# First in-projection of a hybrid encoder as Strassen's seven products, tokens fed in columns

## The chip, the cores and the metric

One core of one Trainium2 chip. The metric is the device time of one execution in microseconds (us); a few runs were made of each kernel, and their median is quoted.

## The reference

Two layers over 2,304 tokens (2,048 of one request, 256 of another) of width 1,024. The part around the change is the first layer's input projection, the rest uses its results:

```python
h = rmsnorm(x, attn_norm[j])          # x * rsqrt(mean(x*x) + eps) * g
proj = h @ w_in                       # (2304 x 1024) @ (1024 x 4096)
q, k, v, z = jnp.split(proj, 4, axis=-1)
# then differential attention of q, k, v; gate by silu(z); output projection;
# then a Fourier layer of the same make
```

All of it is float32 in and out.

## The kernel before, in words

The kernel is a sequence of stages with a barrier between them; a tile's name begins with its stage: `ia` (this projection), `pa` (attention), `oa` (its output projection), `fg` and `fl` (the Fourier layer's gate and transform), `of` (the last output projection). Each engine has its instructions written out in program order; semaphores alone tie the engines together. Float32 accuracy comes from three passes (`three_pass`, lines 206 to 208): each operand is kept as a rounded high part and the rest, its low part, and high x high, low x high and high x low are added in PSUM.

`project_resident` is the stage that is replaced. SP loads 18 blocks of 128 tokens in rows. For each, ACT squares and sums a row and takes the root (lines 442, 444), DVE inverts it, POOL scales the row by it (line 357), PE transposes it (line 399), DVE multiplies by the norm's weight on its way out of PSUM (line 483), ACT rounds it to `xh` (449), and DVE (488) or POOL (361) subtracts to get `xl`. All tokens then stay in SBUF. The weights come in 32 blocks of 128 columns, 512 KB each, loaded by POOL's own DMA queue; POOL makes both parts of each (lines 348 and 352). For each block there are five groups of tokens, four of 512 and one of 256, each of 8 x 3 matmuls. ACT copies a result out of PSUM (line 463, with Silu for `z`), for q and k DVE subtracts to get the low part (line 505), and SP stores. The first groups of tokens are multiplied while later ones are still being made.

## Time and profile before

| | us |
|---|---|
| median of 3 runs | 3052.32 (3045.8 to 3053.98) |
| profiled execution, first to last instruction (its span) | 3051.8 |
| PE busy | 2933.4 (96%) |
| PE weight loads | 2465.4 (81%) |
| DVE busy | 1464.9 (48%) |
| ACT busy | 1339.9 (44%) |
| POOL busy | 790.1 (26%) |

The span is that of the profiled execution; its device time is not listed apart from the three, and the nearest of these is 3052.32, 0.5 above the span. Matmuls are pipelined and their recorded durations overlap, so a rate is read from the distance between starts, not from a duration. Busy shares are means over the stages.

### The profile page before, as it was taken

To read this page: it belongs to the slowest core of one execution; us is meant where nothing else is said; L and a number is where in the kernel's file an instruction comes from. 1 tells how busy PE (TensorE), PEld (TensorE's weight loads), DVE (VectorE), ACT (ScalarE), POOL (GpSimd) and SP (SyncE) were. 2 spreads that over 40 slices of the span, in tenths; PEclk is the share of its full clock that TensorE was granted. 3 is DMA by queue.
4 is the path that set the end of the run, shared out by engine and by line. 5 is a ranking of instruction groups with operands and counts; after the bars stand their busy time and mean duration, and the time that the engine had idled before them with its cause. 6 is when DMAs were issued, how large, how long until landed. Compare 5 with 4: busy or idle time off the path is not lost. (4 is left out here: it accounts for less than half of the span.)

```text
span 3051.8 us, 41686 instructions
## 1 busy us (share of the span) xinstructions
PE 2933.4 (96%) x15038; PEld 2465.4 (81%) x15038; DVE 1464.9 (48%) x1678; ACT 1339.9 (44%) x2348; POOL 790.1 (26%) x414
## 2 busy tenths in 40 slices
PE   7999999999989999999999999998899899899799
PEld 6888888888868787878787888887688899887687
DVE  5111110000068787878787878887787200441322
ACT  6111111111167777777777777775443321221321
POOL 6211111111012222222222222222665221130642
PEclk9999999999989999999999999999899999999899
DMA  6333332242155313232323222120664622565752
GB/s 212 131 114 120 113 107 71 67 116 69 54 135 163 85 56 75 67 71 63 78 63 75 67 61 72 36 88 25 215 207 153 216 91 76 151 172 177 264 177 106
DMA packets 225779, 340.22 MB, mean 111 GB/s; under 512 B 21819, under 2 KB 171515, under 8 KB 220124
## 3 DMA queue, kind: packets, MB, share of 16 engines
q1 hardware_dynamic: 220860, 320.96, 33.5%
q0 software_dynamic: 4736, 16.91, 2.1%
q8 instruction: 103, 1.69, 0.2%
q14 instruction: 80, 0.66, 0.1%
HBM read 224.55 MB, written 125.97 MB: 115 GB/s over the span
## 5 line engine op out<-in xcount | busy, mean ns | idle before, releaser
L1017 DVE TENSOR_REDUCE pa_half_max<-pa_score 128x1 f32<-128x1024 f32 x512 | 625.4, 1222 | 232.5 <-PE pa_score L805 232.5
L951 ACT ACTIVATE pa_p<-pa_score,pa_neg_max 128x1024 f32<-128x1024 f32 x512 | 567.9, 1111 | 75.1 <-DVE pa_neg_max L1023 71.5
L864 PE MATMUL pa_o_acc<-pa_wt,pa_vv 128*128 128x256 f32 x2048 | 511.5, 380 | 1.0 <-ACT pa_o_out_s L986 0.3
L1108 POOL TENSOR_SCALAR pa_p<-pa_p,pa_inv_sum,pa_lam_neg 128x2048 f32<-128x2048 f32 x128 | 262.7, 2052 | 944.7 <-DVE pa_inv_sum L1044 944.7
L801 PE MATMUL pa_score<-pa_ka,pa_qa 128*128 128x512 f32 x1024 | 455.1, 444 | 20.4 <-ACT pa_p L951 9.9
L206 PE MATMUL ia_acc<-ia_xh,ia_wh 128*128 128x512 f32 (+1 forms) x1280 | 472.0, 369 | 1.1 <-DVE ia_stage L505 1.1
L207 PE MATMUL ia_acc<-ia_xl,ia_wh 128*128 128x512 f32 (+1 forms) x1280 | 471.4, 368 | 0.0
L208 PE MATMUL ia_acc<-ia_xh,ia_wl 128*128 128x512 f32 (+1 forms) x1280 | 471.1, 368 | 0.0
L805 PE MATMUL pa_score<-pa_kb,pa_qb 96*128 96x512 f32 x1024 | 422.0, 412 | 0.0
L931 ACT ACTIVATE pa_wt<-pa_turned 128x512 f32<-128x512 f32 x512 | 306.0, 598 | 260.4 <-PE pa_turned L833 259.2
L864 PEld LDWEIGHTS pa_o_acc<-pa_wt,pa_vv 128*128 128x128 f32 x2048 | 367.4, 191 | 44.9 <-ACT pa_o_out_s L986 2.1
L463 ACT ACTIVATE ia_stage<-ia_acc 128x512 fp32r<-128x512 f32 (+3 forms) x160 | 89.0, 556 | 662.0 <-PE ia_acc L208 648.6
L833 PE MATMUL pa_turned<-pa_ident,pa_p 128*128 128x128 f32 x2048 | 314.7, 276 | 10.5 <-ACT pa_wt L931 9.5
L833 PEld LDWEIGHTS pa_turned<-pa_ident,pa_p 128*128 128x128 f32 x2048 | 238.7, 140 | 90.3 <-ACT pa_wt L931 49.4
L1055 DVE SCALAR_TENSOR_TENSOR pa_p<-pa_p,pa_inv_sum 128x2048 f32<-128x2048 f32 x128 | 300.3, 2346 | 0.1
L206 PEld LDWEIGHTS ia_acc<-ia_xh,ia_wh 128*128 128x128 f32 x1280 | 241.6, 189 | 41.7 <-ACT ia_stage L463 1.3
L207 PEld LDWEIGHTS ia_acc<-ia_xl,ia_wh 128*128 128x128 f32 x1280 | 241.6, 189 | 39.9
L208 PEld LDWEIGHTS ia_acc<-ia_xh,ia_wl 128*128 128x128 f32 x1280 | 241.4, 189 | 40.1
L801 PEld LDWEIGHTS pa_score<-pa_ka,pa_qa 128*128 128x128 f32 x1024 | 196.1, 191 | 64.7 <-ACT pa_p L951 20.6
L805 PEld LDWEIGHTS pa_score<-pa_kb,pa_qb 96*128 96x128 f32 x1024 | 196.3, 192 | 32.8
L505 DVE TENSOR_TENSOR ia_stage<-ia_acc,ia_stage 128x512 fp32r<-128x512 f32 (+1 forms) x80 | 51.0, 638 | 319.2 <-ACT ia_stage L463 319.2
L526 DVE TENSOR_TENSOR pa_lam_prod<-pa_lam_vec 128x128 f32<-128x128 f32 x1 | 0.3, 291 | 407.2 <-DMA pa_lam_vec<-attn_lambda_k 407.2
(260 smaller groups left out, 4173.0 us busy)
## 6 DMA issues: line engine op xcount, KB each, us to landing
ia_raw<-attn_w_in POOLq DMA_DIRECT2D x32, 512.0 KB, 4.7
qk_hi<-ia_stage SPq DMA_DIRECT2D x64, 256.0 KB, 2.0
qk_lo<-ia_stage SPq DMA_DIRECT2D x64, 256.0 KB, 2.1
pa_ka<-qk_hi SPq DMA_DIRECT2D x32, 512.0 KB, 6.5
fl_slices<-normed SPq DMA_DIRECT2D x26, 512.0 KB, 6.5
pa_vt<-v SPq DMA_DIRECT2D x8, 1152.0 KB, 6.7
x<-oa_x SPq DMA_DIRECT2D x18, 512.0 KB, 2.9
normed<-oa_h_out SPq DMA_DIRECT2D x9, 1024.0 KB, 5.4
```

What stands on the lines that cost most here:

```text
L206: pe.matmul(out, a_hi(k), b_hi(k), start=first and n == 0, stop=False)
L207: pe.matmul(out, a_hi(k), b_lo(k), start=False, stop=False)
L208: mm = pe.matmul(out, a_lo(k), b_hi(k), start=False, stop=last and n == len(ks) - 1)
L801: pe.matmul(out[:, c], qa[s][:, n, at:at + P], ka[hs][:, n, cols], start=True, stop=False)
L805: mm = pe.matmul(out[:, c], qb[s][:, n, at:at + P], kb[hs][n][:, cols], start=False, stop=True)
L833: mm = pe.transpose(turned[:, x * P:(x + 1) * P], src, ident[:])
L864: mm = pe.matmul(o_acc[:], vv[:, k], wt[:, g % 2, k], start=k == 0, stop=k == NB - 1)
L931: act.activation(wt[:, s, 4 * c:4 * c + 4, at:at + P], turned[:].rearrange("p (k t) -> p k t", k=4), ACT.Copy).then_inc(turned_out, 1)
L951: act.activation(dst[:, half * HALF:(half + 1) * HALF], score[:, (4 * q + j) % RING].rearrange("p a b -> p (a b)"), ACT.Exp, bias=neg_max[ ...
L1017: dve.tensor_reduce(half_max[:, q % 2, n, half:half + 1], score[:, (4 * q + j) % RING].rearrange("p a b -> p (a b)"), AX_X, ALU.max).then_ ...
L1055: dve.scalar_tensor_tensor(out=a, in0=a, scalar=inv_sum[:, par, 0:1], in1=p1[:, par], op0=ALU.mult, op1=ALU.add).then_inc(weights, 1)
L1108: pool.tensor_scalar(p1[:, par], p1[:, par], inv_sum[:, par, 1:2], lam["neg"][:, 0:1], ALU.mult, ALU.mult).then_inc(p1_scaled, 1)
```

## The change

`project_quads` takes the stage's place. The tokens come from the host as columns (`x_cols`), so nothing is transposed on the chip. The work is cut into 3 spans of 768 tokens (two halves of 384 columns) and, in each span, 16 pairs of weight blocks: 48 quads. A quad is a two by two block product: the inner dimension is halved as well (`HALF_K` is 4), and its four results `C21, C12, C11, C22` of 128 x 384 are made from seven products instead of eight, in the order M2, M4, M1, M3, M5, M7, M6. Each product is 4 x 3 matmuls of 384 columns. Five of the seven need a sum of two weight blocks (POOL, `weight_sum`), five need a sum of two token blocks, made once for each span (`x_add`: on DVE in the first span; in the others one on DVE, four on POOL). ACT rounds each factor, DVE subtracts for its low part (`weight_low`, `x_low`). The weights are loaded, added and split anew in every span, through a ring of 10 slots.

Out of PSUM, ACT copies four products, POOL joins two pairs, DVE adds or subtracts six times from PSUM. The norm's factor of a token is no longer in the tokens: squares are added by POOL, summed over partitions by a matmul with ones, and each result is multiplied by `rstd` (three by DVE, one by POOL). For q and k, two low parts each are made by DVE and by POOL. In each span but the last, the next span's tokens are loaded, squared and weighed during pairs j = 2 to 9 (q and k are j = 0 to 7). Weights and stores are issued by SP.

```diff
-def project_resident(nc, tag, w_dram, norm_dram, ident_dram, sections, source, copies, arena, ahead):
...
+COLS = 3 * P
+T_PAIR = 2 * COLS
+SPANS = T // T_PAIR
+W_PAIRS = 2 * HEADS
+QUADS = SPANS * W_PAIRS
+HALF_K = KB // 2
...
+def project_quads(nc, tag, w_dram, norm_dram, sections, x_cols, copies, arena, ahead):
...
+    SETS = 7
+    RING = 10
+    BANKS = 8
+    SUMMED = (0, 2, 4, 5, 6)
...
+        xh = m.sb("xh", [P, SETS, HALF_K, COLS], F32R)
+        xl_at = (nc.sbuf_base + 31) // 32 * 32
+        xl = m.sb("xl", [P, SETS, HALF_K, COLS], F32R)
+        x_sums = nc.alloc_sbuf_tensor_at("ia_x_sums", [P, SETS, HALF_K, COLS], F32, offset=xl_at)
+        wh = m.sb("wh", [P, RING, HALF_K, P], F32R)
+        wl_at = (nc.sbuf_base + 31) // 32 * 32
+        wl = m.sb("wl", [P, RING, HALF_K, P], F32R)
+        w_sums = nc.alloc_sbuf_tensor_at("ia_w_sums", [P, RING, HALF_K, P], F32, offset=wl_at)
+        raw = m.sb("raw", [P, 2, KB, 2 * P])
...
+        M2, M4, M1, M3, M5, M7, M6 = range(SETS)
+        C21, C12, C11, C22 = range(4)
...
+        def w_terms(n, i):
+            return ((w_part(n, 1, 0), w_part(n, 1, 1), ALU.add), (w_part(n, 1, 1),), (w_part(n, 0, 0), w_part(n, 1, 1), ALU.add),
+                    (w_part(n, 0, 0),), (w_part(n, 0, 0), w_part(n, 0, 1), ALU.add),
+                    (w_part(n, 0, 1), w_part(n, 1, 1), ALU.subtract), (w_part(n, 1, 0), w_part(n, 0, 0), ALU.subtract))[i]
...
+        def x_terms(i):
+            return ((x_part(0, 0),), (x_part(1, 0), x_part(0, 0), ALU.subtract), (x_part(0, 0), x_part(1, 1), ALU.add),
+                    (x_part(0, 1), x_part(1, 1), ALU.subtract), (x_part(1, 1),), (x_part(1, 0), x_part(1, 1), ALU.add),
+                    (x_part(0, 0), x_part(0, 1), ALU.add))[i]
...
+        def pool_adds(p, i):
+            return p > 0 and i > 1
...
+                def load_weights(n):
+                    if n < QUADS:
+                        sp.wait_ge(w_lo, SETS * (n - 2) + SETS)
+                        at = (n % W_PAIRS) * 2 * P
+                        sp.dma_start(raw[:, n % 2], w_dram[0].rearrange("(k p) n -> p k n", p=P)[:, :, at:at + 2 * P]).then_inc(raw_in[n % 2], 16)
...
+                def weight_sum(s):
+                    n, i = divmod(s, SETS)
+                    if n >= QUADS or i not in SUMMED:
+                        return
+                    pool.wait_ge(raw_in[n % 2], 16 * (n // 2 + 1))
+                    wait(pool, products, s - RING + 1)
+                    x, y, op = w_terms(n, i)
+                    pool.tensor_tensor(w_sums[:, s % RING], x, y, op).then_inc(w_sum, 1)
+                def add_square(p, e):
+                    pool.wait_ge(squared, 8 * p + e + 1)
+                    total = squares[:, e // 4]
+                    if e % 4:
+                        wait(pool, square_added, 6 * p + 3 * (e // 4) + e % 4 - 1)
+                        pool.tensor_tensor(total, total, square[:], ALU.add).then_inc(square_added, 1)
+                    if e % 4 == 3:
+                        pool.wait_ge(square_added, 6 * p + 3 * (e // 4) + 3)
+                        pool.tensor_tensor(total[:, 0], total[:, 0], total[:, 1], ALU.add).then_inc(square_folded, 1)
+                def x_add(p, i):
+                    pool.wait_ge(products, SETS * W_PAIRS * p - SETS + i + 1)
+                    pool.wait_ge(weighted, units_needed(p, i))
+                    x, y, op = x_terms(i)
+                    pool.tensor_tensor(x_sums[:, i], x, y, op).then_inc(x_sum_pool, 1)
...
+                for slot in range(LAST + 4):
+                    n, t = divmod(slot, SETS)
+                    p, j = divmod(n, W_PAIRS)
+                    if n < QUADS:
+                        if t == 3:
+                            pool.wait_ge(copies_out, 4 * n + 2)
+                            pool.tensor_tensor(tile(n, C21), tile(n, C21), tile(n, C11), ALU.add).then_inc(joined, 1)
+                        if t == 4:
+                            pool.wait_ge(copies_out, 4 * n + 3)
+                            pool.tensor_tensor(tile(n, C11), tile(n, C11), tile(n, C22), ALU.add).then_inc(joined, 1)
+                        if t == 5:
+                            pool.wait_ge(joined, 2 * n + 1)
+                            pool.wait_ge(inverted, 2 * p + 1)
+                            pool.tensor_tensor(tile(n, C21), tile(n, C21), rstd[:, p % 2, 0], ALU.mult).then_inc(scaled_pool, 1)
+                    if n and t == 0 and kind_of(n - 1) == "split":
+                        pool.wait_ge(out_hi, acts_before(n - 1) + C21 + 1)
+                        pool.tensor_tensor(tile(n - 1, C21).bitcast(F32R), tile(n - 1, C21), f32(tile_hi(n - 1, C21)),
+                                           ALU.subtract).then_inc(out_lo_pool, 1)
+                    if n and t == 2 and kind_of(n - 1) == "split":
+                        pool.wait_ge(out_hi, acts_before(n - 1) + C11 + 1)
+                        pool.tensor_tensor(tile(n - 1, C11).bitcast(F32R), tile(n - 1, C11), f32(tile_hi(n - 1, C11)),
+                                           ALU.subtract).then_inc(out_lo_pool, 1)
+                    ahead_set = slot - SETS * W_PAIRS * (p if j < 8 else p + 1) + 6
+                    span = p if j < 8 else p + 1
+                    if 0 < span < SPANS and ahead_set in X_SUMMED and pool_adds(span, ahead_set):
+                        x_add(span, ahead_set)
+                    if p + 1 < SPANS and 2 <= j < 10 and t == 6:
+                        add_square(p + 1, j - 2)
+                    weight_sum(slot + 9)
...
+                def wait_bank(x):
+                    if place_no[x] < BANKS:
+                        return
+                    q, i = places[place_no[x] - BANKS][-2:]
+                    if places[place_no[x] - BANKS][0] == "squares":
+                        pe.wait_ge(rooted, 2 * q + i + 1)
+                    elif i in (M4, M1):
+                        pe.wait_ge(copies_out, 4 * q + i + 1)
                     else:
...
+                        pe.wait_ge(fused, 6 * q + {M2: 1, M5: 3, M3: 4, M7: 5, M6: 6}[i])
+                def multiply(n, i):
+                    s, p = SETS * n + i, n // W_PAIRS
+                    pe.wait_ge(w_lo, s + 1)
+                    if n % W_PAIRS == 0:
+                        pe.wait_ge(x_lo, SETS * p + i + 1)
+                    wait_bank((n, i))
+                    three_pass(pe, bank(n, i), lambda k: wh[:, s % RING, k], lambda k: wl[:, s % RING, k],
+                               lambda k: xh[:, i, k], lambda k: xl[:, i, k], range(HALF_K)).then_inc(products, 1)
+                def sum_squares(p, half):
+                    pe.wait_ge(square_folded, 2 * p + half + 1)
+                    wait_bank(("squares", p, half))
+                    pe.matmul(bank_of(("squares", p, half)), ones[:], squares[:, half, 0], start=True, stop=True).then_inc(square_summed, 1)
...
+                def take(n, i, k):
+                    act.wait_ge(products, SETS * n + i + 1)
+                    if i == M2:
+                        wait(act, stored[n % 2], stored_before(n))
+                    act.activation(tile(n, k), bank(n, i), ACT.Copy).then_inc(copies_out, 1)
...
+                def weigh(p, e):
+                    half, kk = unit_at(p, e)
+                    dve.wait_ge(squared, 8 * p + e + 1)
+                    for k in range(2 * kk, 2 * kk + 2):
+                        x = dve.tensor_scalar(h[:, k, half], h[:, k, half], norm_w[:, k:k + 1], None, ALU.mult)
+                    x.then_inc(weighted, 1)
+                def weight_low(s):
+                    n, i = divmod(s, SETS)
+                    if n >= QUADS:
+                        return
+                    dve.wait_ge(w_hi, s + 1)
+                    src = w_sums[:, s % RING] if i in SUMMED else w_terms(n, i)[0]
+                    dve.tensor_tensor(wl[:, s % RING], src, f32(wh[:, s % RING]), ALU.subtract).then_inc(w_lo, 1)
+                def x_add(p, i):
+                    wait(dve, products, SETS * W_PAIRS * p - SETS + i + 1)
+                    dve.wait_ge(weighted, units_needed(p, i))
+                    x, y, op = x_terms(i)
+                    dve.tensor_tensor(x_sums[:, i], x, y, op).then_inc(x_sum, 1)
+                def x_low(p, i):
+                    dve.wait_ge(x_hi, SETS * p + i + 1)
+                    src = x_sums[:, i] if i in X_SUMMED else x_terms(i)[0]
+                    dve.tensor_tensor(xl[:, i], src, f32(xh[:, i]), ALU.subtract).then_inc(x_lo, 1)
...
+                for slot in range(LAST + 4):
+                    n, t = divmod(slot, SETS)
+                    p, j = divmod(n, W_PAIRS)
+                    if n < QUADS:
+                        if t == 5:
+                            dve.wait_ge(joined, 2 * n + 2)
+                            dve.tensor_tensor(tile(n, C22), tile(n, C22), bank(n, M2), ALU.subtract).then_inc(fused, 1)
+                            dve.wait_ge(products, SETS * n + M5 + 1)
+                            dve.wait_ge(copies_out, 4 * n + 4)
+                            dve.tensor_tensor(tile(n, C12), tile(n, C12), bank(n, M5), ALU.add).then_inc(fused, 1)
+                            dve.tensor_tensor(tile(n, C11), tile(n, C11), bank(n, M5), ALU.subtract).then_inc(fused, 1)
+                        if t == 6:
+                            dve.wait_ge(fused, 6 * n + 1)
+                            dve.tensor_tensor(tile(n, C22), tile(n, C22), bank(n, M3), ALU.add).then_inc(fused, 1)
+                            dve.wait_ge(products, SETS * n + M7 + 1)
+                            dve.wait_ge(fused, 6 * n + 3)
+                            dve.tensor_tensor(tile(n, C11), tile(n, C11), bank(n, M7), ALU.add).then_inc(fused, 1)
+                            if n == 0:
+                                invert(0, 0)
+                                invert(0, 1)
+                            scale(n, C12)
+                    if n and t == 0:
+                        scale(n - 1, C11)
+                        dve.wait_ge(products, SETS * n)
+                        dve.wait_ge(fused, 6 * (n - 1) + 4)
+                        dve.tensor_tensor(tile(n - 1, C22), tile(n - 1, C22), bank(n - 1, M6), ALU.add).then_inc(fused, 1)
+                        scale(n - 1, C22)
+                    if n and t == 1:
+                        low(n - 1, C12)
+                    if n and t == 3:
+                        low(n - 1, C22)
+                    if slot < 5:
+                        x_low(0, slot + 2)
+                    if slot in (1, 2):
+                        x_add(0, slot + 4)
+                    span = p if j < 8 else p + 1
+                    ahead_set = slot - SETS * W_PAIRS * span + 6
+                    if 0 < span < SPANS and ahead_set in X_SUMMED and not pool_adds(span, ahead_set):
+                        x_add(span, ahead_set)
+                    ahead_set = slot - SETS * W_PAIRS * span + 4
+                    if 0 < span < SPANS and 0 <= ahead_set < SETS:
+                        x_low(span, ahead_set)
+                    if p + 1 < SPANS and 2 <= j < 10 and t == 6:
+                        weigh(p + 1, j - 2)
+                    if p + 1 < SPANS and j == 11 and t in (3, 6):
+                        invert(p + 1, t // 6)
+                    weight_low(slot + 7)
...
+    tokens = np.concatenate([np.asarray(inputs["x_prompt"])[0], np.asarray(inputs["x_sample"])[0]])
+    x_cols = feed("x_cols", tokens.T.reshape(KB, P, T))```

How it moves instructions. POOL in the middle of q and k; before, the loop over weight blocks, where one block of two instructions serves 5 groups of 512 or 256 tokens (`raw` is the loaded weight, `products` PE's progress):

```order
L341 DMA ia_raw<-attn_w_in 128x8x128
L57 REGISTER_ALU
L57 ISA [waits ia_products]
L348 CAST ia_wh<-ia_raw 128x1024 [waits ia_raw_in0]
L351 REGISTER_ALU
L352 TENSOR_TENSOR ia_wl<-ia_raw,ia_wh 128x1024 [waits ia_w_hi]
```

and of the change, one quad of q and k (`c` holds the results, `hi` their rounded part):

```order
L490 TENSOR_TENSOR ia_c<-ia_c,ia_hi 128x384 [waits ia_out_hi]
L442 TENSOR_TENSOR ia_w_sums<-ia_raw 128x512 [waits ia_products,ia_raw_in0]
L494 TENSOR_TENSOR ia_c<-ia_c,ia_hi 128x384 [waits ia_out_hi]
L442 TENSOR_TENSOR ia_w_sums<-ia_raw 128x512 [waits ia_products,ia_raw_in0]
L480 TENSOR_TENSOR ia_c<-ia_c 128x384 [waits ia_copies_out]
L442 TENSOR_TENSOR ia_w_sums<-ia_raw 128x512 [waits ia_products,ia_raw_in0]
L483 TENSOR_TENSOR ia_c<-ia_c 128x384 [waits ia_copies_out]
L442 TENSOR_TENSOR ia_w_sums<-ia_raw 128x512 [waits ia_products,ia_raw_in0]
L487 TENSOR_TENSOR ia_c<-ia_c,ia_rstd 128x384 [waits ia_inverted,ia_joined]
```

POOL now has ten two-input instructions in each such quad (a fifth `w_sums` stands ahead of these rows), and a quad is a 48th of the stage. DVE in the same place; before, the low parts of the results, and next to nothing else:

```order
L52 ISA [waits ia_out_hi]
L505 TENSOR_TENSOR ia_stage<-ia_acc,ia_stage 128x512 [waits ia_stored0]
L503 REGISTER_ALU
L505 TENSOR_TENSOR ia_stage<-ia_acc,ia_stage 128x512 [waits ia_stored1,ia_out_hi]
L503 REGISTER_ALU
```

and of the change, from the middle of one quad into the next (`acc` is PSUM):

```order
L715 TENSOR_TENSOR ia_c<-ia_c,ia_acc 128x384 [waits ia_joined]
L718 TENSOR_TENSOR ia_c<-ia_c,ia_acc 128x384 [waits ia_copies_out,ia_products]
L719 TENSOR_TENSOR ia_c<-ia_c,ia_acc 128x384
L659 TENSOR_TENSOR ia_wl<-ia_w_sums,ia_wh 128x512 [waits ia_w_hi]
L722 TENSOR_TENSOR ia_c<-ia_c,ia_acc 128x384 [waits ia_fused]
L725 TENSOR_TENSOR ia_c<-ia_c,ia_acc 128x384 [waits ia_fused,ia_products]
L681 TENSOR_TENSOR ia_c<-ia_c,ia_rstd 128x384 [waits ia_fused,ia_inverted]
L659 TENSOR_TENSOR ia_wl<-ia_w_sums,ia_wh 128x512 [waits ia_w_hi]
L681 TENSOR_TENSOR ia_c<-ia_c,ia_rstd 128x384 [waits ia_fused,ia_inverted]
L734 TENSOR_TENSOR ia_c<-ia_c,ia_acc 128x384 [waits ia_fused,ia_products]
```

A whole quad of q and k has 18 instructions on DVE: 6 that read PSUM, and 12 whose two inputs both lie in SBUF (7 `wl`, 3 by `rstd`, 2 low parts). At the stage's start DVE stands in this order, where a piece of the tokens was read out of PSUM before:

```order
L650 TENSOR_SCALAR ia_h<-ia_h,ia_norm_w 128x384 [waits ia_squared]
L650 TENSOR_SCALAR ia_h<-ia_h,ia_norm_w 128x384
L665 TENSOR_TENSOR ia_x_sums<-ia_h 128x1536 [waits ia_weighted]
L659 TENSOR_TENSOR ia_wl<-ia_raw,ia_wh 128x512 [waits ia_w_hi]
L670 TENSOR_TENSOR ia_xl<-ia_x_sums,ia_xh 128x1536 [waits ia_x_hi]
```

Of the 1536-element rows there are 12 on DVE before the last product of the first quad can start.

## Rows read from the trace of the kernel before

**Rows 1.** The profile's page, part 4, the chain that ended last

```profile
PE 11%; DMA 1%; issue 1%; POOL 1%; ACT 0%; DVE 0%; SPq 0%; ACTq 0%; DVEq 0%; POOLq 0%
```

**Rows 2.** Stretches (from:to, length, busy of each engine, clock, DMA share, GB/s)

```profile
75.00:440.00 365.00, 364.19 (x1787) 308.98 (x1785) 49.14 (x77) 42.44 (x76) 67.86 (x48) 1.00 0.35 119
...
835.00:856.00 21.00, 11.33 (x38) 7.74 (x37) 6.08 (x12) 4.17 (x7) 2.18 (x4) 0.75 0.65 162
...
2398.00:2598.00 200.00, 200.00 (x1153) 199.67 (x1152) 10.62 (x7) 46.01 (x69) 46.32 (x16) 1.00 0.32 110
```

**Rows 3.** Timeline, PE in `ia` (start, length, instruction): first product, last ones, next stage

```profile
34.80 0.77 PE L206 MATMUL ia_acc<-ia_xh,ia_wh 128*128 128x512 f32 x1
...
828.01 0.39 PE L206 MATMUL ia_acc<-ia_xh,ia_wh 128*128 128x512 f32 x1
...
832.09 0.28 PE L206 MATMUL ia_acc<-ia_xh,ia_wh 128*128 128x256 f32 x1
...
834.85 0.28 PE L208 MATMUL ia_acc<-ia_xh,ia_wl 128*128 128x256 f32 x1
...
839.23 0.47 PE L801 MATMUL pa_score<-pa_ka,pa_qa 128*128 128x512 f32 x1 [0.90 <-PEq L87]
```

**Rows 4.** Groups by line and form, DVE and POOL (busy us, mean ns; idle before)

```profile
L1718 POOL TENSOR_TENSOR fg_xl<-fg_h_in,fg_xh 128x1536 fp32r<-128x1536 f32 x10 | 35.1, 3515 | 107.7 <-ACT fg_xh L1751 107.7
L505 DVE TENSOR_TENSOR ia_stage<-ia_acc,ia_stage 128x512 fp32r<-128x512 f32 x64 | 44.2, 691 | 287.7 <-ACT ia_stage L463 287.7
L2377 DVE TENSOR_TENSOR fl_mix<-fl_mix 128x1024 f32<-128x1024 f32 x8 | 9.8, 1220 | 0.2
L1772 DVE MEMSET fg_stage<- 128x384 f32 x1 | 0.4, 378 | 1.9 <-PEq L87 1.9
```

**Rows 5.** Timeline, POOL and DVE alone: a 384 and a 1024 on POOL, a 1024 on DVE

```profile
2394.87 1.00 POOL L1714 TENSOR_TENSOR fg_xl<-fg_h_in,fg_xh 128x384 fp32r<-128x384 f32 x1 [41.70 <-ACT fg_xh L1759]
...
44.73 2.40 POOL L361 TENSOR_TENSOR ia_xl<-ia_h,ia_xh 128x1024 fp32r<-128x1024 f32 x1
...
34.91 1.22 DVE L488 TENSOR_TENSOR ia_xl<-ia_h,ia_xh 128x1024 fp32r<-128x1024 f32 x1
36.05 0.16 DVE L475 RECIPROCAL ia_rstd<-ia_root 128x1 f32<-128x1 f32 x1
```

**Rows 6.** Timeline, DVE and POOL at once, both with two inputs in SBUF (stages `oa`, `fg`)

```profile
2140.01 3.35 POOL L1320 TENSOR_TENSOR oa_wl<-oa_raw,oa_wh 128x1024 fp32r<-128x1024 f32 x1
2143.33 3.36 POOL L1320 TENSOR_TENSOR oa_wl<-oa_raw,oa_wh 128x1024 fp32r<-128x1024 f32 x1
...
2153.70 3.43 DVE L1530 TENSOR_TENSOR oa_wl<-oa_raw,oa_wh 128x1024 fp32r<-128x1024 f32 x1
...
2397.82 3.94 POOL L1714 TENSOR_TENSOR fg_xl<-fg_h_in,fg_xh 128x384 fp32r<-128x384 f32 x2
...
2399.76 2.00 POOL L1714 TENSOR_TENSOR fg_xl<-fg_h_in,fg_xh 128x384 fp32r<-128x384 f32 x1
```

**Rows 7.** Timeline at the start: a DVE that reads PSUM beside a POOL

```profile
15.03 1.20 POOL L357 TENSOR_SCALAR ia_xr<-ia_xr,ia_rstd,ia_one 128x1024 f32<-128x1024 f32 x1 [1.32 <-DVE ia_rstd L475]
...
14.85 1.20 DVE L483 TENSOR_TENSOR ia_h<-ia_acc,ia_norm_w 128x1024 f32<-128x1024 f32 x1
```

**Rows 8.** Groups by line and form, ACT, and DVE's long reciprocal, PE's float32 matmul

```profile
L463 ACT ACTIVATE ia_stage<-ia_acc 128x512 fp32r<-128x512 f32 x64 | 38.3, 599 | 299.9 <-PE ia_acc L208 299.9
L1756 ACT ACTIVATE fg_stage<-fg_acc 128x384 f32<-128x384 f32 x48 | 23.6, 492 | 145.4 <-PE fg_acc L208 144.8 <-DMA fnet_gate<-fg_stage 0.4
L1535 DVE RECIPROCAL oa_sq<-oa_sq 128x512 f32<-128x512 f32 x32 | 106.3, 3339 | 8.2 <-ACT oa_sq L1439 8.2
L1733 PE MATMUL fg_acc<-fg_stage 128*128 128x384 f32 x6 | 4.0, 831 | 3.6 <-DVE fg_stage L1772 3.6
```

**Rows 9.** The timeline's first data in (ACT's first instruction), and the page's weight loads

```profile
4.48 1.28 ACT L442 ACT_TABLE_LOAD   x1 [4.48 <-DMA ia_xr<-x_prompt]
...
ia_raw<-attn_w_in POOLq DMA_DIRECT2D x32, 512.0 KB, 4.7
```

496 lines of the change are left out of this document (270 added, 226 removed).

## Prediction

> **What bounds the kernel now.** I read the chain that ended last, then the stretches, the timeline of the stage's first and last products, then the prices of single instructions. The chain is PE's wherever it is named with a weight [rows 1]. In the stage that is replaced PE is the bound outright: 364.2 us busy out of 365 at full clock, while DVE and POOL work 49 and 68 us [rows 2]. The first product starts at 34.8, the last ends at 834.85 + 0.28 = 835.1, and the next stage's first matmul starts 4.1 us later [rows 3]. So whatever moves the end of this stage moves the end of the kernel, nearly one for one. Reading the starts: 18 matmuls of 512 columns between 828.01 and 832.09, 0.227 us each [rows 3]. The gate stage has the same three passes at 384 columns: 1,153 in 200.0 us, 0.1735 us each, although its weight loads are busy 199.7 of 200 [rows 2]. Fewer columns for each weight load thus costs only what the columns cost.
>
> **PE's part.** 48 quads x 7 products x 12 matmuls = 4,032, at 0.1735 us: 700 us, 14.6 us a quad and 2.1 us a product. Six float32 matmuls with ones come to it, 0.83 each [rows 8], 5 us. Before, products and transposes fill the 800.3 us from 34.8 to 835.1. If nothing else held PE, the stage would gain some 95 us. What the change adds is on the other engines, so I price a quad there.
>
> **ACT** has 7 roundings of 512 and 8 instructions of 384 at most: 7 x 0.60 + 8 x 0.49 [rows 8] = 8.1 us of 14.6. It never decides.
>
> **DVE and POOL alone.** POOL: 384 elements 1.00, 1024 elements 2.40 [rows 5], 1536 elements 3.52 [rows 4]: a line of 0.16 + 2.19 ns an element, so 512 is 1.28 and 768 is 1.84. DVE: 512 is 0.69, 1024 is 1.22 [rows 4]: 384 is 0.56, 1536 is 1.75. A quad of q and k has on POOL 5 x 1.28 + 5 x 1.00 = 11.4 us, on DVE 7 x 0.69 + 11 x 0.56 = 11.0. Each by itself fits into 14.6. A quad of v or z has two low parts fewer on either: 9.4 and 9.9.
>
> **DVE and POOL together.** This is where I expect the gain to go. With both at two-input work in SBUF, POOL's 1024 takes 3.35 and starts every 3.32 us, DVE's takes 3.43 [rows 6], against 2.40 and 1.22 alone [rows 5]. A pair of them costs 3.32 where the sum is 3.62; POOL's 384 beside DVE's 1024 starts every 1.94 [rows 6], where the sum is 2.22. So they take turns, and 0.28 us is hidden each time they alternate. A DVE instruction that reads PSUM is not held: 1.20 beside a POOL instruction of 1.20 [rows 7]. Two DVE instructions in a row start 1.14 apart, 0.08 less than their length [rows 5].
>
> So the six PSUM readers of a quad are free of this, and the port, as I call what the two share, carries for q and k: POOL 11.4, and DVE 7 x 0.69 + 5 x 0.56 = 7.6, together 19.0; less 10 alternations of 0.28 and 2 x 0.08: 16.0. I add 0.3 (between 0 and 1, no row shows it) for instructions that wait on their own engine's last result: **16.3 us against PE's 14.6**. For v and z: 9.4 + 6.5 = 15.9, less 8 x 0.28 and 2 x 0.08: 13.5, so PE decides, 14.6. Bounds for the 16.3: 15.5, if the 0.16 fixed part of every one of the 22 is hidden, and 19.0 if nothing is; the pairs stand between and nearest.
>
> The Trainium skill's "SBUF — State Buffer" (section "SBUF: two separate sides") says that GpSimd and a VectorE instruction with two SBUF inputs share a pair of ports under an exclusive lock, and that the loser blocks for the whole instruction. By that rule a quad of q and k would be the plain sum, 19.0; rows 6 say blocked, but with 0.28 given back at each turn, and I go by them.
>
> PE runs ahead only as far as the ring and the eight banks let it: M2's bank is wanted 8 products on, and DVE frees it in the sixth slot, behind POOL's second joining. That is a lead of some 3 products, 6 us: it moves the stall, and doesn't remove one that comes in every quad.
>
> **Ahead work.** In j = 2 to 9 of spans 0 and 1 the next 768 tokens are prepared: POOL 6 x 1.84 + 2 x 1.00 = 13.0, DVE 16 multiplications of 384 by the norm's weight. The trace has none of this form; the nearest is DVE's memset of 384, 0.38 [rows 4], the ends are nothing and the two-input 0.56. 6.1 us. Less 8 alternations: 16.9 for 8 quads, 2.1 each. So 6 quads at 18.4 and 2 (v) at 13.5 + 2.1 = 15.6.
>
> **Between spans** seven sets of tokens are replaced within some nine products: POOL 4 x 3.52, DVE 8 x 1.75, less 4 alternations: 27.0 us. The quad's own spare 1.1 and the lead of 6, regained in the PE-bound quads, come off: 19.5 to 20, twice. I take 19.5.
>
> **The first quad.** Before its last product DVE has 16 x 0.38 + 12 x 1.75 + 11 x 0.69 = 34.7, POOL 6 x 1.84 + 2 x 1.00, 10 sums at 1.28 and 2 joinings, 27.8: 62.5, less about 20 alternations, 56.9. Tokens land at 4.5 [rows 9]. So the last product starts at 61.4 and ends at 63.5. DVE then has two reciprocals of 384, 3.34 x 0.75 = 2.5 each [rows 8], of which I let 3 show: 66.5. Before, the first product stood at 34.8; here the early products run meanwhile, but the stage cannot get ahead of the last one.
>
> **The sum.** Span 0: 66.5 + 16.3 + 6 x 18.4 + 2 x 15.6 + 6 x 14.6 + 19.5 = 331.5. Span 1: 2 x 16.3 + 110.4 + 31.2 + 87.6 + 19.5 = 281.3. Span 2: 8 x 16.3 + 8 x 14.6 = 247.2. Four of the float32 matmuls in PE-bound quads, 3.3. Products end at 863.3, against 835.1: +28.2. Behind the last product DVE adds, scales and ACT does the Silu before the store, where ACT did it alone: two short instructions more, 2 x 0.56, and a wait between them, +1.5. Nothing behind the stage is changed. 3051.8 + 29.7 = 3081.5; the median of the runs is 0.5 above the span: **3082 us**.
>
> Costed at nothing: the transposes that go (they lay in the 800.3 already), and the weights' reloading, 50 MB instead of 17, issued by SP between the stores. Its cover: the DMA engines' share was 0.35 in this stage [rows 2], 512 KB landed 4.7 us after issue [rows 9], so some 9 for 1 MB, and between the store that it stands behind and POOL's first sum of it lie four products' time, 9 us, with POOL's own lead of nine slots over PE behind that. Without the cover it is a rival below.
>
> **The rivals.** A measurement of this kernel tells about 0.3% from no change, 9 us.
>
> *PE decides in every quad (faster).* If a turn hides more than 0.28 for these shorter instructions, so that 16.0 falls below 14.6, that is 0.42 a turn, the q and k quads run at PE's pace and ahead work too. For it: the lead, the spread of the instructions over seven slots, and that no row shows 384 against 512. Against: two forms that differ in length by 2.7 times gave 0.30 and 0.28. Then 66.5 + 47 x 14.6 + 2 x 19.5 + 3.3 = 795, 40 us under before, 3013. If the port were no limit at all, the first quad would be DVE's 34.7 alone and nothing would be lost between spans: 2950.
>
> *The port costs its lower bound (about the same).* 15.5 a quad, the norm's multiplications free: 11 quads 0.8 less, 12 quads 1.6 less, the first 8 less: 36 less than my sum, 3046.
>
> *Nothing is hidden (much slower).* 19.0 and 15.9 a quad, 21.4 and 18.3 with ahead work, 72 for the first, 28 between spans: products end near 985, 3204.
>
> *The weights come late.* POOL stands in order: a wait for the load also holds its joinings, and through them DVE and PE. Each us of it in every quad would be 47 us: 3130 for one.
>
> *PE's clock.* The gaps of some us between spans may drop it: in the 21 us behind the stage it was 0.75 [rows 2]. PE isn't the bound there, so 5 us at a span's change, inside the range.
>
> **How the numbers follow.** Forecast 0.55, of it 0.05 between 3043 and 3061; PE decides 0.25; lower bound 0.10, of it 0.08 within 9 us; nothing hidden 0.03; late weights 0.07. Faster 0.25 + 0.02 = 0.27, same 0.05 + 0.08 = 0.13, slower the rest, 0.60. Half of PE's case and the two dearest, some 0.2, lie outside the range. The range reaches from PE's case, 3013, to late weights, 3135. The forecast's own range is 3055 to 3115.
>
> **What would show it.** In the new profile: 384-column matmuls 0.1735 us apart inside a product; q and k quads every 16 to 16.6 us (18.4 with ahead work), v and z quads every 14.6; DVE's 512 subtraction at a mean well over 0.69, near 1.2, POOL's 512 sum over 1.28, the PSUM readers at 0.56; PE's idle put down to DVE's `ia_c`, `ia_wl` or to POOL; the last product of the first quad near 61. It would be wrong if DVE's two-input instructions kept to 0.69 beside a busy POOL, or if PE's waits named DMA.

## The result, and the profile after

| | us |
|---|---|
| before, median of 4 runs beside it | 3052.04 (3045.8 to 3053.98) |
| changed kernel, median of 4 runs | 3155.04 (3151.96 to 3161.53) |
| ratio, 95% interval | 1.0347 [1.0329, 1.0364] |
| span of the profiled execution, before and after | 3051.8 and 3156.0 |

The change costs 103 us; the forecast was 30. The direction was right. The size was not, and 3155 lies above the range, which ended at 3135. In the runs on record the device time is 1.6 to 2.2 us above the span, and not 0.5 as the forecast took it; that is too little to matter here.

The stretches of the stage come first, as far as the account below needs it: the start, the quads with ahead work, PE-bound quads, the change of span, the q and k quads of span 2, its v and z quads, and what follows the stage.

```profile
0.00:82.00 82.00, 32.66 (x139) 30.28 (x140) 67.37 (x54) 32.09 (x43) 39.31 (x29) 0.79 0.26 84
82.00:268.00 186.00, 153.56 (x803) 150.55 (x801) 179.73 (x182) 72.82 (x144) 145.25 (x102) 0.91 0.49 148
268.00:329.00 61.00, 55.30 (x303) 54.36 (x303) 58.42 (x67) 28.69 (x54) 42.74 (x30) 0.94 0.55 167
329.00:404.00 75.00, 58.38 (x290) 56.74 (x288) 74.14 (x59) 32.93 (x53) 64.41 (x33) 0.84 0.28 81
...
714.00:833.00 119.00, 103.70 (x588) 101.67 (x588) 118.27 (x126) 51.36 (x105) 98.81 (x71) 1.00 0.52 153
833.00:938.00 105.00, 100.71 (x576) 99.86 (x577) 96.72 (x115) 43.49 (x86) 75.14 (x52) 1.00 0.49 142
...
938.40:960.00 21.60, 10.15 (x35) 7.14 (x34) 6.97 (x14) 4.31 (x7) 2.33 (x4) 0.74 0.70 179
```

Against [rows 2], where PE was busy 364 us of 365, PE now has gaps in every stretch, and DVE is the engine that has hardly any: 118.27 of 119 in the q and k quads, 74.14 of 75 at the change of span. From the start to 938 PE works 761 us in the changed kernel; before it was 814 up to 835. So the change did take 53 us off PE's busy time. PE then waits: of the 938 us it is idle 177. The 761 are still 56 more than the 705 that the forecast gave to PE's work. The granted clock averaged 0.92 over the 938 us, a mean of times at 2.4 and at 1.2 GHz, where it was 1.00 before: it was lower at the start, in the ahead quads and at the change of span (0.79, 0.91, 0.84), and PE's matmuls took longer there.

PE's timeline at the end of the stage and at the start of the next:

```profile
937.50 0.33 PE L206 MATMUL ia_acc<-ia_xh,ia_wh 128*128 128x384 f32 x1
937.68 0.33 PE L207 MATMUL ia_acc<-ia_xl,ia_wh 128*128 128x384 f32 x1
937.85 0.33 PE L208 MATMUL ia_acc<-ia_xh,ia_wl 128*128 128x384 f32 x1
938.02 2.59 PE L540 MATMUL ia_acc<-ia_xh,ia_wh 128*128 128x384 f32 x14
...
943.07 0.47 PE L1050 MATMUL pa_score<-pa_ka,pa_qa 128*128 128x512 f32 x1 [2.45 <-PEq L87]
```

(L540 is a run of 14 matmuls whose result nobody uses; the kernel before has them too.) The last product ends at 937.85 + 0.33 = 938.2, against 835.1 [rows 3]: 103.1 us later. The spans differ by 104.2. The loss is thus in this stage, all but 1.1 us. Starts are 0.17 to 0.18 apart, as priced.

What PE and its weight loads wait for, up to 960, in total, times and longest:

```profile
PE ia_acc L206 <- DVE ia_c L715: 102.7, 32, 6.1
PE ia_acc L206 <- DVE ia_xl L670: 49.3, 5, 19.8
PE ia_acc L206 <- issue: 23.1, 8, 7.8
...
PEld ia_acc L206 <- DVE ia_wl L659: 113.1, 34, 6.3
```

The same idle time shows on both queues, so the lines are not to be added. Every large one that names an engine names DVE (`issue`, 23.1 on PE and 77.6 on its weight loads, is time for which the profile shows no wait): the subtraction that frees M2's bank (L715), the weights' low parts (L659), the tokens' low parts (L670). None names a DMA. And the groups by form, up to 960:

```profile
L659 DVE TENSOR_TENSOR ia_wl<-ia_w_sums,ia_wh 128x512 fp32r<-128x512 f32 x240 | 311.9, 1300 | 0.8 <-ACT ia_wh L560 0.8
...
L681 DVE TENSOR_TENSOR ia_c<-ia_c,ia_rstd 128x384 f32<-128x384 f32 x144 | 132.0, 917 | 5.8 <-DVE ia_c L734 1.0
...
L686 DVE TENSOR_TENSOR ia_c<-ia_c,ia_hi 128x384 fp32r<-128x384 f32 x48 | 72.1, 1503 | 0.0
...
L650 DVE TENSOR_SCALAR ia_h<-ia_h,ia_norm_w 128x384 f32<-128x384 f32 x48 | 58.6, 1262 | 20.0 <-ACT ia_square L547 10.1 <-DMA ia_norm_w<-attn_norm 7.1 <-ACT ia_squares L547 2.8
...
L670 DVE TENSOR_TENSOR ia_xl<-ia_x_sums,ia_xh 128x1536 fp32r<-128x1536 f32 x15 | 40.0, 2668 | 0.9 <-ACT ia_xh L571 0.9
...
L715 DVE TENSOR_TENSOR ia_c<-ia_c,ia_acc 128x384 f32<-128x384 f32 x48 | 26.1, 544 | 11.5 <-POOL ia_c L483 11.5
...
L442 POOL TENSOR_TENSOR ia_w_sums<-ia_raw 128x512 f32<-128x512 f32 x240 | 384.4, 1605 | 86.2 <-PE ia_acc L208 53.5 <-DMA ia_raw<-attn_w_in 32.7
...
L458 POOL TENSOR_TENSOR ia_x_sums<-ia_h 128x1536 f32<-128x1536 f32 x8 | 33.0, 4134 | 0.0
```

DVE's 512 takes 1.30 where it takes 0.69 alone [rows 4], POOL's 512 1.61 where the line through its other lengths gives 1.28, POOL's 1536 4.13 for 3.52. The PSUM reader L715 keeps to 0.54. These are the lengths that the prediction expects of a shared port; the experiments below test it.

**The account.** I set the starts of DVE's last addition of a quad (M6, L734) against the forecast's sum. "Ahead" are the eight quads in which the next tokens are prepared.

| piece | forecast | measured | surplus |
|---|---|---|---|
| first quad to its last addition | 66.5 | 81.3 | 14.8 |
| quads 1 and 17 | 2 x 16.3 | 18.1 + 17.1 | 2.6 |
| ahead, quads 2 to 9 and 18 to 25 | 2 x 141.6 | 163.3 + 162.3 | 42.4 |
| five PE-bound quads, twice | 2 x 73.0 | 73.3 + 73.5 | 0.8 |
| last quad of a span and first of the next, twice | 2 x 50.4 | 56.9 + 57.0 | 13.1 |
| span 2, seven q and k quads | 114.1 | 119.5 | 5.4 |
| span 2, v and z | 116.8 | 116.0 | -0.8 |
| float32 matmuls | 3.3 | in the rows above | -3.3 |
| sum (before rounding) | 863.3 | 938.2 | 74.9 |

More than half of the miss is in the ahead quads. A quad is counted here from one M6 addition to the next, and a q or k quad's two low parts on DVE and one of its two on POOL are made behind its own M6 addition. So the first v quad of a span still carries these of the k quad before it. Quad 8, from 222.12 to 244.03, has them; one of DVE's is this:

```profile
224.67 1.64 DVE L686 TENSOR_TENSOR ia_c<-ia_c,ia_hi 128x384 fp32r<-128x384 f32 x1
```

The forecast priced this quad as a v quad without them. Two of the ahead quads, in ACT's timeline:

```profile
154.17 0.85 ACT L547 ACTIVATE ia_square<-ia_h 128x768 f32<-128x768 f32 x1 [7.32 <-DMA ia_h<-x_cols]
...
174.85 0.84 ACT L547 ACTIVATE ia_square<-ia_h 128x768 f32<-128x768 f32 x1 [7.09 <-DMA ia_h<-x_cols]
```

and the issue of the second one's tokens on SP's queue:

```profile
166.95 0.78 SPq L397 DMA_DIRECT2D qk_hi<-ia_hi  x1
168.94 0.33 SPq L402 DMA_DIRECT2D qk_lo<-ia_c  x1
169.31 0.59 SPq L374 DMA_DIRECT2D ia_h<-x_cols  x1
```

ACT reaches the squares 7 us before the tokens are there. SP issues their load only behind the last stores of the quad before. ACT stands in order, and behind the squares stand its weight roundings and the copies out of PSUM. That wait is not in my sum: I had costed the loads that SP issues for the weights, not the one for the tokens.

### The profile page after: what moved, and what is told of

Read it like the earlier page. It is cut to its first block and busy times, and to the rows that moved or that the text cites. A ratio compares the mean times of both kernels' runs of the same rounds, so it can differ in the third digit from the quotient of the medians.

```text
span 3156.0 us, 43070 instructions
## 1 busy us (share of the span) xinstructions
PE 2880.2 (91%) x15098; PEld 2519.9 (80%) x15098; DVE 2268.1 (72%) x2448; ACT 1595.6 (51%) x2838; POOL 1321.8 (42%) x758
## 5 line engine op out<-in xcount | busy, mean ns | idle before, releaser
L206 PE MATMUL ia_acc<-ia_xh,ia_wh 128*128 128x384 f32 x1344 | 475.1, 354 | 175.7 <-DVE ia_c L715 102.7
L1050 PE MATMUL pa_score<-pa_ka,pa_qa 128*128 128x512 f32 x1024 | 456.8, 446 | 21.3 <-ACT pa_p L1200 9.6
L207 PE MATMUL ia_acc<-ia_xl,ia_wh 128*128 128x384 f32 x1344 | 468.2, 348 | 0.0
L208 PE MATMUL ia_acc<-ia_xh,ia_wl 128*128 128x384 f32 x1344 | 467.3, 348 | 0.0
L442 POOL TENSOR_TENSOR ia_w_sums<-ia_raw 128x512 f32<-128x512 f32 x240 | 384.4, 1605 | 86.2 <-PE ia_acc L208 53.5
L206 PEld LDWEIGHTS ia_acc<-ia_xh,ia_wh 128*128 128x128 f32 x1344 | 267.1, 199 | 191.3 <-DVE ia_wl L659 113.1
L659 DVE TENSOR_TENSOR ia_wl<-ia_w_sums,ia_wh 128x512 fp32r<-128x512 f32 x240 | 311.9, 1300 | 0.8 <-ACT ia_wh L560 0.8
L207 PEld LDWEIGHTS ia_acc<-ia_xl,ia_wh 128*128 128x128 f32 x1344 | 267.2, 199 | 0.7
L208 PEld LDWEIGHTS ia_acc<-ia_xh,ia_wl 128*128 128x128 f32 x1344 | 266.7, 198 | 0.0
L1050 PEld LDWEIGHTS pa_score<-pa_ka,pa_qa 128*128 128x128 f32 x1024 | 196.7, 192 | 66.7 <-ACT pa_p L1200 21.0
L560 ACT ACTIVATE ia_wh<-ia_w_sums 128x512 fp32r<-128x512 f32 x240 | 149.5, 625 | 178.5 <-POOL ia_w_sums L442 178.0
## 6 DMA issues: line engine op xcount, KB each, us to landing
pa_ka<-qk_hi SPq DMA_DIRECT2D x32, 512.0 KB, 6.5
fl_slices<-normed SPq DMA_DIRECT2D x26, 512.0 KB, 6.5
```

The source lines that it names most:

```text
L206: pe.matmul(out, a_hi(k), b_hi(k), start=first and n == 0, stop=False)
L207: pe.matmul(out, a_hi(k), b_lo(k), start=False, stop=False)
L208: mm = pe.matmul(out, a_lo(k), b_hi(k), start=False, stop=last and n == len(ks) - 1)
L442: pool.tensor_tensor(w_sums[:, s % RING], x, y, op).then_inc(w_sum, 1)
L659: dve.tensor_tensor(wl[:, s % RING], src, f32(wh[:, s % RING]), ALU.subtract).then_inc(w_lo, 1)
L1050: pe.matmul(out[:, c], qa[s][:, n, at:at + P], ka[hs][:, n, cols], start=True, stop=False)
```

## The experiments

All are edits of the changed kernel, of 3155.0 us. The kernel before, run beside them, had medians of 3047.3 to 3052.0 us; the ratios take that out, the differences of medians below do not, and are uncertain by a few us for it. The table gives, from each one's own trace, the same pieces as above: the first quad's last addition, ahead (two spans), change of span (two quads, twice), one q or k quad of span 2 (mean of seven), the last addition of the stage.

| | median us | ratio to before | first | ahead | change of span | q/k | last |
|---|---|---|---|---|---|---|---|
| changed kernel | 3155.0 | 1.0347 [1.0329, 1.0364] | 81.3 | 163.3, 162.3 | 56.9, 57.0 | 17.1 | 938.2 |
| e1 sums out | 3045.2 | 0.9979 [0.9968, 0.9990] | 71.3 | 143.5, 143.1 | 49.9, 49.9 | 13.8 | 827.8 |
| e2 PSUM factor | 3120.2 | 1.0228 [1.0208, 1.0248] | 81.3 | 154.7, 151.6 | 55.0, 54.6 | 16.7 | 902.8 |
| e3 join on DVE | 3120.3 | 1.0228 [1.0208, 1.0248] | 79.6 | 159.0, 159.4 | 54.8, 54.8 | 16.2 | 909.0 |
| e4 into tokens | 3064.8 | 1.0045 [1.0015, 1.0076] | 85.6 | 130.6, 130.5 | 52.8, 52.0 | 14.9 | 850.9 |
| e5 late squares | 3135.8 | 1.0288 [1.0267, 1.0309] | 80.4 | 147.5, 149.8 | 56.9, 56.9 | 17.1 | 917.9 |
| e6 e3 + e4 + e5 | 3020.2 | 0.9899 [0.9875, 0.9923] | 83.3 | 117.3, 117.7 | 51.8, 49.6 | 13.8 | 803.9 |
| e7 e6, start, x sums | 3009.4 | 0.9868 [0.9844, 0.9892] | 79.5 | 118.2, 116.7 | 48.1, 46.0 | 13.9 | 794.6 |
| e8 x sums on DVE | 3143.9 | 1.0313 [1.0292, 1.0334] | 81.0 | 163.3, 162.2 | 51.7, 51.7 | 17.3 | 927.9 |
| e9 norm first | 3149.9 | 1.0341 [1.0323, 1.0359] | 80.8 | 163.1, 162.4 | 56.3, 56.9 | 17.1 | 935.8 |
| e11 e2 + e5 + e8 | 3092.7 | 1.0147 [1.0130, 1.0164] | 81.1 | 141.4, 142.2 | 51.7, 51.4 | 16.8 | 880.5 |
| e12 no norm weights | 3124.8 | 1.0256 [1.0239, 1.0273] | 81.3 | 144.5, 144.1 | 56.9, 56.9 | 17.1 | 909.0 |

**POOL's weight sums left out.**

```diff
-    SUMMED = (0, 2, 4, 5, 6)
+    SUMMED = ()
```

> Left out: the sums of two weight blocks; each factor is rounded and split from one block, so POOL has five instructions fewer in a quad and everything else, all loads, stores, products and DVE's 18 instructions, stays. Port theory (DVE and POOL take turns at what two-input instructions in SBUF use, and the turns set the pace): a q and k quad's port load falls from 19.0 to 12.6 us, less 5 turns of 0.28 = 11.2, under PE's 14.6; quads come every 14.6 to 15 us, DVE's 512 subtraction falls from a mean of 1.3 us towards 0.69; stage end about 780 to 800 instead of 938, so 2990 to 3020. Rival, late transfers (POOL waited 33 us for weights, ACT 115 us for tokens): the loads are the same, so it stays above 3100. Rival, DVE's own instructions and their order are too long: they are unchanged, so it stays within 20 us of 3155.

Without POOL's five sums a quad, a q or k quad takes no more than PE's 14.6 (the 13.8 in the table is a mean in which DVE catches up with PE), and PE is busy 116.56 of 119:

```profile
714.00:833.00 119.00, 116.56 (x672) 116.27 (x671) 73.03 (x121) 48.95 (x97) 28.41 (x25) 1.00 0.51 144
```

POOL's sums, then, are what holds these quads; that it is by the port and not by POOL's own length, the next two runs say. But the time, 3045, is 25 us above the expected range. The ahead quads still take 18 us each with POOL's sums gone, so what holds them is something else. ACT's waits from 82 to 940 in this kernel name it:

```profile
ACT ia_square L547 <- DMA ia_h<-x_cols: 99.4, 12, 9.1
```

This run turned me from "the port costs more than I priced" to "the tokens come late".

**Three multiplications read PSUM.** C12, C11 and C22 are multiplied by a product's bank and not by the factor in SBUF; the values are therefore not the reference's, the number and size of the instructions are kept. Two of the three also stand one place earlier on DVE, and that was not tried by itself.

```diff
-                    dve.tensor_tensor(tile(n, k), tile(n, k), rstd[:, p % 2, half], ALU.mult).then_inc(scaled, 1)
+                    dve.tensor_tensor(tile(n, k), tile(n, k), bank(n, i), ALU.mult).then_inc(scaled, 1)
```

> Changed: DVE's three multiplications of a quad read their second input from a PSUM bank (a product's, not the factor), in the same number and size, two of them a place earlier; the values are those of another factor. Port theory: they leave the port, 3 x 0.56 less in every quad, less the turns that no longer hide 0.28: 0.8 to 1.7 us a quad where the port decides (about 36 quads), so 3095 to 3127, and the mean of these three falls from 0.92 to 0.54 us. Rival, DVE's count and length of instructions decide: both unchanged, 3155 within 10. Rival, transfers: 3155 within 10.

The multiplications fall from 0.92 to 0.54, and 35 us are gained, inside the expectation, with POOL's instructions as they were:

```profile
L685 DVE TENSOR_TENSOR ia_c<-ia_c,ia_acc 128x384 f32<-128x384 f32 x144 | 74.2, 541 | 1.7 <-PE ia_acc L208 1.7
```

**The joinings on DVE, from PSUM.** POOL's two additions a quad of copied products go; DVE adds the bank itself.

```diff
-                        if t == 3:
-                            pool.tensor_tensor(tile(n, C21), tile(n, C21), tile(n, C11), ALU.add).then_inc(joined, 1)
...
+                        if t == 4:
+                            dve.tensor_tensor(tile(n, C21), tile(n, C21), bank(n, M4), ALU.add).then_inc(joined, 1)
...
+                            dve.tensor_tensor(tile(n, C11), tile(n, C11), bank(n, M1), ALU.add).then_inc(joined, 1)
```

> Changed: the two joinings of a quad (C21, C11) are made by DVE, adding M4 and M1 from PSUM, instead of by POOL from SBUF; same results. DVE gets 2 x 0.46 us more work outside the port, POOL 2 x 1.00 less inside. Port theory: 0.5 to 1.4 us less a quad where the port decides, 3105 to 3137. Rival, DVE's own length decides (it has no idle time in the q and k quads): 0.93 more a quad, 3180 to 3200.

DVE has two instructions more in every quad, which hardly stood still before; still the kernel is 35 us faster and a q or k quad 0.9 shorter. That rules out DVE's own length as the bound, and leaves what DVE and POOL share or POOL's own length; against the latter speaks the run above, in which POOL's instructions are unchanged.

**The factor goes into the tokens.** As before the change: squares and roots are done first, and one DVE instruction multiplies each token block by the norm's weight and by the factor; no product is scaled.

```diff
-                        x = dve.tensor_scalar(h[:, k, half], h[:, k, half], norm_w[:, k:k + 1], None, ALU.mult)
+                        x = dve.scalar_tensor_tensor(h[:, k, half], h[:, k, half], norm_w[:, k:k + 1], rstd[:, p % 2, half], ALU.mult, ALU.mult)
...
-                            scale(n, C12)
```

> Changed: the norm's factor goes into the tokens, in the same instruction as its weight, and the four multiplications of a quad's outputs go (three on DVE, one on POOL); squares of the next span are summed at j = 10, its tokens weighed in j = 11 to 14; same results. Port theory: port load of a q and k quad from 19.0 to 16.3, less 9 turns = 13.8, so PE decides there (14.6 to 15 us), 18.5 or less with ahead work; the first product is some 8 us later; in sum 3065 to 3110. Rival, transfers decide: 3140 to 3160. Rival, moved work only comes back in the quads before the change of span: 3120 to 3150.

3064.8, 90 us less than the changed kernel, just under the expected range's lower end. The q and k quads of span 2, where nothing but the multiplications by the factor goes, fall from 17.1 to 14.9, with joinings still on POOL. Of the 90 us, 65 are gained in the ahead quads, and there the run doesn't tell the causes apart: their multiplications go, DVE's weighing is moved behind them (to j = 11 to 14), and ACT's wait for tokens is shorter too. The first quad comes later, 85.6 for 81.3, since the tokens wait for the roots, and so do the five quads behind the ahead ones, 75.9 and 77.7.

**Squares one quad later.**

```diff
-                    if p + 1 < SPANS and 2 <= j < 10 and t == 5:
-                        square_unit(p + 1, j - 2)
+                    if p + 1 < SPANS and 3 <= j < 11 and t == 5:
+                        square_unit(p + 1, j - 3)
```

(so also POOL's sum and DVE's weighing; the loads stay)

> ACT's squares of the next span's tokens, POOL's sums of them and the weighing come one quad later (j = 3 to 10 in place of 2 to 9); the loads of these tokens stay where they are, and nothing else is changed. Late-token theory: ACT stands in order and waits up to 7.3 us for tokens that SP issues behind the stores of the quad before; a quad later they have landed. The wait of ACT's squares on the load, 86.8 us in the changed kernel, goes to under 10, quads with ahead work go from 20.8 to 18.5 or 19, and the time to 3115 to 3130. Port-alone theory: the ahead quads are long because POOL's and DVE's ahead instructions cost more than I priced; their number and neighbours are the same, so 3145 to 3160.

The wait is gone: no line of ACT in this stage names `x_cols` from 82 on, and the squares start without idle time.

```profile
160.35 0.83 ACT L547 ACTIVATE ia_square<-ia_h 128x768 f32<-128x768 f32 x1
...
179.64 0.83 ACT L547 ACTIVATE ia_square<-ia_h 128x768 f32<-128x768 f32 x1
```

19 us are gained, clearly more than the rival's none, but less than the 25 to 40 that I expected. The ahead pieces of the table fall by 28, of which 8 come back in the five quads behind them, where the last ahead quad now stands. The 16 quads with ahead work now take 18.8 us on average where they took 20.4. The ten of q and k among them are at 18.9, which is 1.8 above the plain 17.06 and near the 2.1 that I had priced; the six of v are at 18.6, for 15.6 forecast, so the wait was not all that is wrong with those. The edit also moves one ahead quad of each span from q to v, worth some 2 us in all by the forecast's own prices (18.4 - 16.3 against 15.6 - 14.6).

**Squares late, joinings on DVE, factor in the tokens.** The three edits above in one kernel; the weighing stands in j = 12 to 14.

> Three edits at once: the norm's factor goes into the tokens (as before the change), so that no product is scaled; the additions that join the products are made by DVE from PSUM, so that POOL joins nothing; the squares come a quad later. The port then carries in a quad of q and k POOL 5 x 1.28 and DVE 7 x 0.69 alone, 11.2 us, in place of 19.0. Port theory: PE decides, 14.6 us, in every quad but those with ahead work (14.6 to 16) and the two between spans (still some 25 us lost each); the first product quad still ends late, near 80 us. 3005 to 3020, below the kernel before. Theory that DVE's own length decides once the port is free (DVE has 7 x 0.69 + 9 readers of PSUM and of SBUF at 0.56): also under 14.6, so the two agree here; what would speak against both is a q and k quad of over 15 us.

3020.2, at the upper end of the expected range, and 30 us under the kernel before as run beside it (3050.0). A q or k quad takes no more than PE's own time, as in e1, and an ahead quad 14.7.

**The same, with another start and all token sums on DVE.** At the start the weights are split before the tokens' norm is waited for, and the second matrix is loaded behind the first tokens.

```diff
         def pool_adds(p, i):
-            return p > 0 and i > 1
+            return False
...
+                for s in range(4):
+                    weight_low(s)
```

> The kernel of the label e6_tokens_join_late with two more edits: at the start the weights are split before the tokens' norm is waited for, and the second matrix is loaded behind the first tokens; and the sums of the token quarters of spans 1 and 2, four of 1536 elements on POOL and the rest on DVE, are all made by DVE. Port theory: a DVE sum of 1536 costs the port 1.75 us where POOL's costs 3.52, so each change of span gives back 5 to 7 us, the start 5 to 10: 2980 to 2995. Rival, that a change of span is DVE's chain and not the port: it gets longer by 4 x 1.75 us there, and the time is that of the other kernel less only the start, 3000 to 3015.

3009.4, the fastest kernel here. The port's range is missed and the rival's, 3000 to 3015, is met, but only as a number: it had each change of span get longer, and each is 3.7 and 3.6 us shorter, if not the 5 to 7 of the port. What is left there is DVE's time, as its share says (no run tried it):

```profile
525.00:580.00 55.00, 43.85 (x226) 41.98 (x225) 55.00 (x57) 28.01 (x45) 27.02 (x14) 0.91 0.30 95
```

DVE 55.00 of 55, POOL 27. The start gave 3.8 at the first quad. In the middle PE has no gap at all:

```profile
618.00:758.00 140.00, 140.00 (x810) 140.00 (x809) 115.96 (x159) 67.59 (x130) 81.73 (x59) 1.00 0.67 192
```

**Token sums on DVE alone.** The edit of `pool_adds` from that diff, by itself on the changed kernel.

> The changed kernel with one edit: the sums of the token quarters of spans 1 and 2 that POOL makes (four of 1536 elements a span) are made by DVE. Port theory: each costs the port 1.75 us where it cost 3.52, 7 us less at each change of span, so 3138 to 3148. Rival, DVE's own length decides there: DVE gets 7 us more at each change, 3160 to 3170.

3143.9, in the port's range: DVE has 7 us more to do at each change of span, and each is 5.2 us shorter. Here, with the products' multiplications in it, POOL and DVE are both full (in the changed kernel 52 and 60 of the 60 us from 654 to 714, the second change), and the cheaper place for a sum is the one that counts.

**The norm's weights loaded first.**

```diff
+                    if e == 0:
+                        sp.dma_start(norm_w[:], norm_dram).then_inc(consts_in, 16)
                     load_unit(0, e)
-                    if e == 0:
-                        sp.dma_start(norm_w[:], norm_dram).then_inc(consts_in, 16)
```

> The changed kernel with one edit: SP loads the norm's weights (4 KB) ahead of the first tokens, not behind them. In the changed kernel DVE starts its first multiplication at 8.08, when the norm's weights have landed, although the first tokens are there at 5.56. Late-constant theory: the start is one chain on DVE, so the first quad's last addition, at 81.27 there, comes 2 to 3 us earlier, and the time is 3151 to 3154. Rival, that the squares (ACT, POOL in turn) set the pace of the start: the last addition stays between 80.5 and 82, and the time too.

Neither theory is settled. The edit only moved the wait to the tokens: ACT starts on them at 8.4 and not at 5.6, and DVE's first multiplication, behind ACT's squares of them, starts at 10.60 instead of 8.08.

```profile
10.60 2.95 DVE L650 TENSOR_SCALAR ia_h<-ia_h,ia_norm_w 128x384 f32<-128x384 f32 x4 [9.58 <-ACT ia_squares L547]
```

The first quad's last addition comes at 80.8 all the same. So DVE starts 2.5 us later here, and the end of the quad doesn't move with it: it rather speaks for the rival. An earlier start was not obtained. Most of the 5 us in the median come from the sitting: the kernel before had 3047.3 beside it, and the ratios differ by 0.0006.

**Three edits together.** e2, e5 and e8 in one kernel (values as in e2).

> Three of the edits together on the changed kernel: the products are multiplied by the factor as they come from PSUM (label e2_psum_factor, 34.9 us less by itself), the squares come a quad later (e5_late_squares, 19.2 less), and DVE makes the token sums of spans 1 and 2 (e8_xadd_dve, 11.1 less). The norm's factor is still in the outputs. If the three stalls lie at different places, as the account of the quads has it, the gains add up: 3155 - 65 = 3090, 3080 to 3100. If they are one stall seen three times, the best of them stands: 3110 to 3120.

3092.7: 62.4 us gained where the three alone gave 34.9 + 19.2 + 11.1 = 65.2. The stalls lie in different places and nearly add up. In the traces, the stage's last addition comes 57.7 us earlier, where the three alone gave 35.4 + 20.3 + 10.3 = 66.0.

**The norm's weights on 8 columns of 384.** e5 with most of that multiplication left out in spans 1 and 2.

```diff
-                        x = dve.tensor_scalar(h[:, k, half], h[:, k, half], norm_w[:, k:k + 1], None, ALU.mult)
+                        part = h[:, k, half] if p == 0 else h[:, k, half, 0:8]
+                        x = dve.tensor_scalar(part, part, norm_w[:, k:k + 1], None, ALU.mult)
```

> The kernel of the label e5_late_squares, where DVE's multiplications of the tokens by the norm's weights in spans 1 and 2 take 8 of the 384 columns: most tokens stay without their weight. These 32 instructions were priced at 0.38 us each, 0.76 a quad, 12 us in all; in the changed kernel they take 1.26 us each. If they need the port as two-input instructions do, a quad with ahead work gets 0.8 to 1.5 us shorter: 3112 to 3124. If they don't need the port, and only DVE's length counts in that they are short, the 16 quads get at most 0.3 shorter: 3131 to 3137. If what they are held for is lost to the quad in full, 2.5 us a quad: 3096 to 3100.

11.0 us less than e5 by the medians, 8.9 by the last addition of the stage: 0.6 to 0.7 for each of 16 quads, near the 0.76 that I had priced from DVE's memset, and 0.8 us outside the range that I gave for the port. The instruction is recorded at 1.26 us, but a quad doesn't lose that. What is left of it isn't free, so this is what the columns cost and a lower bound for the whole: even with 8 columns it takes 0.67 us:

```profile
L651 DVE TENSOR_SCALAR ia_h<-ia_h,ia_norm_w 128x8 f32<-128x8 f32 x32 | 20.1, 670 | 0.0
```

## Why the prediction was right in sign and wrong in size

**PE's part held where PE had no gaps.** Matmuls start 0.17 to 0.18 us apart; the five PE-bound quads of a span took 73.3 and 73.5 for 73.0, v and z 116.0 for 116.8. PE's busy time did fall, and the added work took it back, as forecast.

**The port held, a little dearer.** A q or k quad of span 2 takes 17.05 to 17.07 us, for 16.3 forecast; e1, e3 and e2 each take a part of its load away and shorten it. The missing 0.8 can be read from POOL's timeline in one such quad:

```profile
751.31 1.29 POOL L442 TENSOR_TENSOR ia_w_sums<-ia_raw 128x512 f32<-128x512 f32 x1
755.48 1.21 POOL L494 TENSOR_TENSOR ia_c<-ia_c,ia_hi 128x384 fp32r<-128x384 f32 x1 [2.88 <-ACT ia_hi L597]
```

POOL stands for 2.88 us. It waits for ACT's rounding of C11. DVE's multiplication of C11 (753.54) stands in order behind a held one of C12 (751.33, 1.69 long). ACT, too, had stood 3.81 us for the one of C12, and then does two weight roundings and a copy before it rounds C11 at 754.89. Meanwhile DVE uses the port alone and turns of 0.28 are not gained. I had added 0.3 for waits in such chains, between 0 and 1; if the rest of that sum holds, it is 1.1. The runs show the size; the cause in this chain is read from the trace, and was not tried by itself. Over the 11 q and k quads without ahead work that is 8 us of the miss, and under the 12 ahead quads of q and k some 9 more.

The Trainium skill's "SBUF — State Buffer" (section "SBUF: two separate sides") lets the loser block for the whole instruction; by that the plain sum of a quad was 19.0. Measured is 17.06, so the rule's plain sum is still too dear, and this in spite of the 2.88 us in which POOL stood. The same section exempts a DVE instruction with at most one SBUF input, outside the modes in which one instruction uses both ports. With the other input in PSUM the runs agree: the last addition of a quad took 0.54 to 0.55 in all 48 cases, and e2, where an operand moved to PSUM, is 35 us faster.

**The step that failed is "Ahead work"**: 2.1 us a quad on top of the plain one, 18.4 and 15.6, which is 17.7 on average. Measured is 20.4, 42 of the 75 us missed. The prices of the instructions were about right (e5: 1.8 for 2.1 in q and k quads; e12: 0.6 to 0.7 for 0.76). What was missing is a wait, a term that the sum put at nothing: the tokens' load stands on SP behind the stores of the quad before, and ACT stands in front of it with its own queue behind. e5 takes it away and gives 19 us. Some 9 are the dearer plain quad. The remaining 14 are not separated. Of the 42, 19 lie in the four v quads with ahead work: forecast was 15.6 for each, and in span 0 they took 21.9 and 18.7 (starts of the last addition 222.12, 244.03, 262.68). One part is known: the first of the two still carries three low parts of a k quad, which the forecast left out. What else makes them long stays open; they are long in e5 too, without the wait.

**The first quad**, 81.3 for 66.5. Its sum went by what DVE and POOL have to do, 56.9 us from the first token on. DVE's timeline shows what was left out:

```profile
8.08 0.75 DVE L650 TENSOR_SCALAR ia_h<-ia_h,ia_norm_w 128x384 f32<-128x384 f32 x2 [7.05 <-DMA ia_norm_w<-attn_norm]
11.76 2.29 DVE L650 TENSOR_SCALAR ia_h<-ia_h,ia_norm_w 128x384 f32<-128x384 f32 x2 [2.93 <-ACT ia_square L547]
...
67.67 1.75 DVE L670 TENSOR_TENSOR ia_xl<-ia_x_sums,ia_xh 128x1536 fp32r<-128x1536 f32 x1
...
69.94 0.54 DVE L715 TENSOR_TENSOR ia_c<-ia_c,ia_acc 128x384 f32<-128x384 f32 x1
...
72.86 4.96 DVE L674 RECIPROCAL ia_rstd<-ia_rstd 128x384 f32<-128x384 f32 x2
77.85 1.33 DVE L681 TENSOR_TENSOR ia_c<-ia_c,ia_rstd 128x384 f32<-128x384 f32 x1
79.10 1.78 DVE L659 TENSOR_TENSOR ia_wl<-ia_w_sums,ia_wh 128x512 fp32r<-128x512 f32 x1
80.80 0.54 DVE L681 TENSOR_TENSOR ia_c<-ia_c,ia_rstd 128x384 f32<-128x384 f32 x1
81.27 0.54 DVE L734 TENSOR_TENSOR ia_c<-ia_c,ia_acc 128x384 f32<-128x384 f32 x1
```

The last low part that the first quad's products need ends at 69.4, 8 us late: DVE starts at 8.08 and not at 4.5, and stands 6.4 us in five gaps for ACT. From there to the addition it is 12 us, of which I had let 5 show: the two reciprocals (4.96), the two multiplications and a low part that stand between them on DVE. In e9 DVE starts 2.5 us later still and the quad ends no later, so the late start may cost nothing by itself; no run made it earlier. The rest is read from the trace.

**Between spans**, 6.5 us too little each, 13 in all. I had deducted a lead of 6 us that PE was to regain. e8 bears out the price of the work itself roughly: by the forecast's prices it takes 4 x (3.52 - 1.75) = 7.1 us of port away, 6.0 when the four turns that go with it are counted, and each change got 5.2 shorter. That the lead doesn't help is an inference from the rest; PE's granted clock was 0.84 at the first change and 0.89 at the second, and not 1.00, so it worked slower as well when it could work; what that cost was not tried.

**The rivals.** PE decides in every quad: no. Nothing is hidden, 3204: no, a quad stays 2 us under its plain sum. The weights come late: no wait of PE in this stage names a DMA. POOL did wait 32.7 us for weights, 8.4 of it at the start and the rest 0.5 to 3.8 at a time; no run takes that away, so that it cost nothing is not shown. This rival's 3130 came nearest to the time. It had the right mechanism, a load behind SP's stores and an engine in order behind it, and the wrong load. Whoever gives a rival to one load on such a queue should give it to every load on it. PE's clock: it fell not only between spans but also in the ahead quads (0.91 and 0.93) and in the first 82 us (0.79). DVE was busy 179.73 of 186 us and 74.14 of 75 in such stretches, so I take the slower PE for a result of its gaps and not for the bound. No run separates the two.

## What to carry to other kernels

- Strassen's seven products save PE an eighth of its matmuls, and cost additions on the engines that had been idle. It paid here (1.0% in e6, 1.3% in e7) only after the norm's factor and the joinings of products had left the port that DVE and POOL share, the factor into the inputs and the joinings with one operand in PSUM, and after the squares no longer waited for their tokens.
- Price additions to an idle engine by what it shares: here POOL's work in SBUF lengthened DVE's 512 subtraction from 0.69 to 1.30 us. Then go through every load that stands behind a store on an in-order queue, and ask which in-order engine stands before it.
- Where several stalls lie at different places, an account by milestones (the start of the same instruction in every quad) tells which term of a sum is off; the busy shares don't.

## What was not expected of the hardware

- DVE can keep POOL out for far longer than one instruction, as the profile has it. In e4, POOL's addition of 384 elements, 1.00 alone [rows 5], took 13.21 us, while DVE ran ten two-input instructions in SBUF back to back; POOL's next one, behind them, took 1.27:

```profile
64.59 13.21 POOL L483 TENSOR_TENSOR ia_c<-ia_c 128x384 f32<-128x384 f32 x1 [10.89 <-ACT ia_c L582]
77.76 1.27 POOL L445 TENSOR_TENSOR ia_w_sums<-ia_raw 128x512 f32<-128x512 f32 x1
```

```profile
64.42 1.75 DVE L661 TENSOR_TENSOR ia_xl<-ia_x_sums,ia_xh 128x1536 fp32r<-128x1536 f32 x1
66.09 1.75 DVE L656 TENSOR_TENSOR ia_x_sums<-ia_h 128x1536 f32<-128x1536 f32 x1
67.76 0.68 DVE L650 TENSOR_TENSOR ia_wl<-ia_raw,ia_wh 128x512 fp32r<-128x512 f32 x1
...
76.24 0.68 DVE L650 TENSOR_TENSOR ia_wl<-ia_w_sums,ia_wh 128x512 fp32r<-128x512 f32 x1
```

  DVE runs at its full pace all that time. So they don't always take turns, as [rows 6] had made me think: here DVE, its next instruction being ready, went first again and again, although POOL's had been waiting. When they alternate and when not is not settled by these runs.
- A DVE instruction with one large input in SBUF and a column of scalars is held beside POOL too: 1.26 us on average in the changed kernel, where its first two take 0.75 together while POOL still waits for its first data, and 0.67 us with 8 columns.
